# Every eighth gathered row added on VectorE instead of TensorE, with the residual rows kept in SBUF

## What is computed

```python
def block(xb):                      # 128 tokens; 8 heads, 16 experts per head
    ...                             # product keys: scores s1, s2, two rounds of top-16
    g = jax.nn.softmax(sc, axis=-1)
    u = jnp.take(u_tab, eidx, axis=0)
    act = jax.nn.gelu(jnp.einsum('thkd,td->thk', u, xb), approximate=False)
    coef = (g * act.astype(jnp.float32)).astype(xb.dtype)
    return jnp.einsum('thk,thkd->td', coef, jnp.take(v_tab, eidx, axis=0))
...
x = x + _peer(_rmsnorm(x, norm_ffn), w_q, keys1, keys2, u_tab, v_tab)
y = _rmsnorm(x, norm_final)
```

## Time and profile before

| | us |
|---|---|
| Median of 3 runs | 3596.52 (3595.49 to 3606.69) |
| The profiled execution | 3593.31 |
| Its span in the trace | 3591.5 |

### The profile page before, as it was taken

The page is one execution under the profiler, slowest core; times in us unless marked ns, Lnnn a source line. Parts: engine busy times, 40 slices in busy tenths (PEclk is TensorE's granted clock), DMA queues, the critical chain, the costliest instruction groups (busy, mean ns, idle before and its releaser), DMA issues.

```text
span 3591.5 us, 33867 instructions
## 1 busy us (share of the span) xinstructions
PE 3193.5 (89%) x10052; PEld 1819.9 (51%) x10052; DVE 2417.2 (67%) x5507; ACT 1431.2 (40%) x4220; POOL 1381.5 (38%) x1231
## 2 busy tenths in 40 slices
PE   7889998999999998999999998989999877777776
PEld 6676555555555555555655555555555322222232
DVE  6633579767656678867656588867656666666664
ACT  4312444554334345554334345553333333333332
POOL 2101345333333445434333345434343444444443
PEclk9899999999999999999999999999999999999999
DMA  4256999999999999999999998999999999999998
GB/s 135 71 170 230 382 418 343 381 415 369 418 411 408 399 411 345 392 392 392 419 405 398 401 407 336 401 386 400 418 411 400 416 419 420 396 420 401 419 381 347
DMA packets 232072, 1336.42 MB, mean 372 GB/s; under 512 B 27664, under 2 KB 49296, under 8 KB 92624
## 3 DMA queue, kind: packets, MB, share of 16 engines
q0 software_dynamic: 156672, 1140.92, 78.1%
q1 hardware_dynamic: 62992, 179.96, 13.5%
q10 hardware_dynamic: 12224, 13.38, 1.0%
HBM read 1310.93 MB, written 23.23 MB: 371 GB/s over the span
## 4 chain that ended last, share of the span: by engine, by line
PE 58%; DMA 21%; DVE 8%; ACT 8%; issue 4%; POOL 1%; POOLq 0%; SPq 0%; ACTq 0%; DVEq 0%
PE ps_acc L765 32%; DMA rows<-in_experts,idx 20%; PE ps_a L593 14%; PE ps_v L593 4%; PE ps_a L668 3%; DVE rows L1383 3%; ACT uy L824 2%; POOL rows L1510 1%; DVE va L1228 1%; ACT coef L918 1%; ACT diag L922 1%; PE ps_a L695 1%; PE ps_y L635 1%; ACT L915 1%; PE ps_a L672 1%
## 5 line engine op out<-in xcount | busy, mean ns | idle before, releaser
L765 PE MATMUL ps_acc<-rows,diag 128*128 128x512 f32 x4352 | 2030.9, 614 | 292.0 <-ACT diag L922 289.3
L1510 POOL DMA_INDIRECT rows<-in_experts,idx x1088 | 1257.3, 1156 | 1894.5 <-PE ps_acc L765 1529.2
L1383 DVE CUSTOM_DVE_ANT_0 rows<-rows,xn 128x1024 f32<-128x1024 f32 x1088 | 1330.1, 1232 | 827.4 <-DMA rows<-in_experts,idx 812.7
L765 PEld LDWEIGHTS ps_acc<-rows,diag 128*128 128x128 f32 x4352 | 831.2, 196 | 1335.8 <-issue 848.0
L915 ACT ACTIVATE act_v<-dots 128x2 f32<-128x2 f32 x544 | 109.6, 201 | 1161.2 <-DVE dots L1383 1150.0
L922 ACT ACTIVATE diag<-pk,coef 128x128 f32<-128x128 f32 x1088 | 377.2, 394 | 17.7
L593 PE MATMUL ps_a<-xnT,ring 128*128 128x272 f32 x1536 | 375.8, 400 | 0.9 <-ACT xnT L812 0.7
L593 PEld LDWEIGHTS ps_a<-xnT,ring 128*128 128x128 f32 x1536 | 297.4, 194 | 93.3 <-issue 34.4
L918 ACT ACTIVATE coef<-act_v,soft 128x1 f32<-128x1 f32 x1088 | 261.4, 287 | 17.8
L593 PE MATMUL ps_a<-gates,ring 128*128 128x272 f32 x1024 | 247.7, 395 | 4.4 <-issue 3.5
L1228 DVE SCALAR_TENSOR_TENSOR va<-va,pk 128x302 f32<-128x302 f32 x480 | 240.2, 564 | 1.9
(11 more groups left out here) (227 smaller groups left out, 2258.9 us busy)
## 6 DMA issues: line engine op xcount, KB each, us to landing
ring<-in_slabs SPq DMA_DIRECT2D x256, 512.0 KB
rows<-in_experts,idx POOLq DMA_INDIRECT x1088
ring<-made_slabs SPq DMA_DIRECT2D x24, 512.0 KB
sc<-score_rows SPq DMA_DIRECT2D x68, 128.0 KB
score_rows<-gp ACTq DMA_DIRECT2D x32, 256.0 KB
xt<-in_x_prompt SPq DMA_DIRECT2D x4, 1024.0 KB, 14.4
x_rows<-xt ACTq DMA_DIRECT2D x4, 1024.0 KB, 10.8
x2t<-x_rows SPq DMA_DIRECT2D x8, 512.0 KB
```

What stands on the lines that cost most here:

```text
L765: ins = pe.matmul(ps_acc[:, h, :], diag[:, slot, :], rows[:, slot, D + h * 512:D + (h + 1) * 512], start=False, stop=False, skip_group_che ...
L1383: ins = dve.tensor_tensor_reduce(rows[:, slot, 0:D], rows[:, slot, 0:D], xn[:, :], 1.0, 0.0, ALU.mult, ALU.add, dots[:, s:s + 1])
L1510: pool.indirect_dma_start(out=rows[:, slot, :], out_offset=None, in_=experts, in_offset=bass.IndirectOffsetOnAxis(ap=idx[:, a, k:k + 1], a ...
```

## The change

The residual rows get two buffers by tile parity (`x2t[:, t % 2, :]`), and stay out of PE: `start` of PE is gone, and PE's first slot of a tile starts the accumulation (`start=first`). In the prompt tiles the slots with s % 8 == 7 (`added`) have no `diag` and no PE product. DVE adds them to `x2t` with one `scalar_tensor_tensor` (`v` half times coefficient plus `x2t`), after the first two dot products of the following turn (after all four in a tile's first turn). This buffer of the ring has a semaphore of its own, `last_free`. At a tile's end DVE adds `ps_acc` and `x2t` into `yt` once both have all slots (`y_sum`), and PE waits for that before its next tile. The squares are then taken from `yt` (ACT, at the end of the tile's first turn), mean and scaling by DVE at the end of turns 1 and 2, and the inverse root is a power on POOL instead of ACT's root and DVE's reciprocal. SP loads rows at turn 3 instead of 1, with another condition, and stores at turn 3 instead of 0.

```diff
+ADDED = RING - 1
-        x2t = sb("x2t", [P, D])
+        x2t = sb("x2t", [P, 2, D])
...
+        def added(n, s):
+            return n < TILES * TPAIRS and s % RING == ADDED
...
             def rows_free(t):
-                sp.wait_ge(acc_begun, t + 1)
-                pass_wait()
-                sp.wait_ge(xn_ready, t + 1)
-                pass_wait()
+                if t >= 2:
+                    sp.wait_ge(y_sq, t - 1)
+                    pass_wait()
...
-                if ended_at(turn) is not None:
-                    store(ended_at(turn))
+                if turn > 32 and turn % 32 == 3:
+                    store(turn // 32 - 1)
...
-            def start(t):
-
-                w = DEC if t == TILES else P
-                pe.wait_ge(x2_in, loads_of(t))
-                pe.wait_ge(y_ready, t + 1)
-                for h in range(2):
-                    last = pe.matmul(ps_acc[:, h, :], eye[0:w, :], x2t[0:w, h * 512:(h + 1) * 512],
-                                     start=True, stop=False, skip_group_check=True)
-                last.then_inc(acc_begun, 1)
...
             def slots(n, s0, s1):
                 for s in range(s0, s1):
-                    slot = s % RING
-                    pe.wait_ge(diag_done, PAIR * n + s + 1)
+                    if added(n, s):
+                        continue
+                    slot, first = s % RING, s == 0 and n % TPAIRS == 0
+                    if first and n:
+                        pe.wait_ge(y_sum, n // TPAIRS)
+                    pe.wait_ge(diag_done, summed(n, s) + 1)
...
-                    ins.then_inc(slot_free, 1)
+                    ins.then_inc(last_free if slot == ADDED else slot_free, 1)
...
             def end_squares(t):
-
-                steps = PAIR * (TILES * TPAIRS + SPAIRS) if t == TILES else PAIR * TPAIRS * (t + 1)
-                act.wait_ge(y_out, 16 * t + 16)
-                act.wait_ge(slot_free, RING + steps)
-                act.activation(yt[:, :], flat(ps_acc[:, :, :]), ACT.Square, accum_out=fin[:, 0:1]).then_inc(y_sq, 1)
+                act.wait_ge(y_sum, t + 1)
+                act.activation(x2t[:, t % 2, :], yt[:, :], ACT.Square, accum_out=fin[:, 0:1]).then_inc(y_sq, 1)
...
+            def add_slot(n, s):
+
+                dve.wait_ge(coef_done, PAIR * n + s + 1)
+                x2 = x2t[:, n // TPAIRS % 2, :]
+                mark(dve.scalar_tensor_tensor(x2, rows[:, ADDED, D:2 * D], coef[:, s:s + 1], x2, ALU.mult, ALU.add))
+                after(count[0])
+                dve.sem_inc(last_free, 1)
...
             def end(t):
...
+                dve.wait_ge(y_out, 16 * t + 16)
...
+                dve.tensor_tensor(yt[:, :], flat(ps_acc[:, :, :]), x2t[:, t % 2, :], ALU.add).then_inc(y_sum, 1)
...
+            def end_scale(t):
+
+                dve.wait_ge(y_std, t + 1)
+                dve.scalar_tensor_tensor(yt[:, :], yt[:, :], fin[:, 2:3], gl[:, :], ALU.mult, ALU.mult).then_inc(y_ready, 1)
...
                     dot(n, STEPS * r, STEPS * r + BATCH)
+                    if added(*earlier):
+                        add_slot(*earlier)
...
+            def end_root(t):
+
+                pool.wait_ge(y_ms, t + 1)
+                pool.tensor_tensor(fin[:, 2:3], fin[:, 1:2], half[:, 0:1], ALU.pow).then_inc(y_std, 1)
...
-                    pool.wait_ge(slot_free, PAIR * n + s + 1)
+                    if slot == ADDED:
+                        pool.wait_ge(last_free, rounds(n, s) + 1)
+                    else:
+                        pool.wait_ge(slot_free, (RING - 1) * rounds(n, s) + slot + 1)
```

More of the change, by code:

```diff
@@ L375, in loads_of, with summed, rounds @@
             return 16 * (TILES + 2) if t == TILES else 16 * t + 16
+        def added(n, s):
+            return n < TILES * TPAIRS and s % RING == ADDED
+        def summed(n, s):
+            whole, part = min(n, TILES * TPAIRS), n - min(n, TILES * TPAIRS)
+            return whole * (PAIR - PAIR // RING) + part * PAIR + (s - s // RING if n < TILES * TPAIRS else s)
+        def rounds(n, s):
+            return PAIR // RING * n + s // RING
         def by_step(ap):
@@ L510, in _ @@
                 beside(2 * turn)
+                if k == 3 and g < GROUPS:
+                    load_rows(2 * g + 1)
                 if k == 1 and g < GROUPS:
-                    load_rows(2 * g + 1)
                     sp.wait_ge(score_out[1], 128 * g + 64)
@@ L774, in _ @@
             pe.wait_ge(kept_in, 16)
-            pe.sem_inc(slot_free, RING)
-            pe.sem_inc(acc_begun, 1)
+            pe.sem_inc(slot_free, RING - 1)
+            pe.sem_inc(last_free, 1)
             pe.sem_inc(y_done, 2)
@@ L788, in _ @@
                     beside(2 * turn + 1)
-                    start(turn // 32)
                     slots(n, s, s + STEPS)
@@ L978, in _ @@
                 if turn % 32 == 0:
-                    if t is not None:
-                        end_squares(t)
                     beside(2 * turn)
-                    if t is not None:
-                        end_root(t)
                     pair_start(n, r)
@@ L990, in _ @@
                 batch(n, TB * r + 1)
+                if t is not None:
+                    end_squares(t)
                 beside(2 * turn + 1)
             end_squares(TILES)
-            end_root(TILES)
         @block.vector
@@ L1401, in end, with end_mean @@
             def end(t):
-                dve.wait_ge(y_sq, 1 * t + 1)
+                last = (LAST_PAIR, PAIR - 1) if t == TILES else (TPAIRS * (t + 1) - 1, PAIR - 2)
+                dve.wait_ge(y_out, 16 * t + 16)
+                dve.wait_ge(slot_free, RING - 1 + summed(*last) + 1 - (rounds(last[0] - TILES * TPAIRS, last[1]) + 1 if t == TILES else 0))
+                dve.wait_ge(last_free, 1 + rounds(*last) + 1)
+                dve.tensor_tensor(yt[:, :], flat(ps_acc[:, :, :]), x2t[:, t % 2, :], ALU.add).then_inc(y_sum, 1)
+            def end_mean(t):
+                dve.wait_ge(y_sq, t + 1)
                 dve.tensor_scalar(fin[:, 1:2], fin[:, 0:1], 1.0 / D, EPS, ALU.mult, ALU.add).then_inc(y_ms, 1)
-                dve.wait_ge(y_std, 1 * t + 1)
-                step(dve.reciprocal(fin[:, 3:4], fin[:, 2:3]))
-                dve.scalar_tensor_tensor(yt[:, :], flat(ps_acc[:, :, :]), fin[:, 3:4],
-                                         gl[:, :], ALU.mult, ALU.mult).then_inc(y_ready, 1)
+            def end_scale(t):
+                dve.wait_ge(y_std, t + 1)
+                dve.scalar_tensor_tensor(yt[:, :], yt[:, :], fin[:, 2:3], gl[:, :], ALU.mult, ALU.mult).then_inc(y_ready, 1)
             setup_constants()
@@ L1432, in _ @@
                     weights(n)
+                earlier = (n, STEPS * r - 1) if r else (n - 1, PAIR - 1)
                 if turn % 32 == 0:
                     dot(n, STEPS * r, STEPS * (r + 1))
+                    if n and added(*earlier):
+                        add_slot(*earlier)
                     if ended_at(turn) is not None:
@@ L1445, in _ @@
                         choose(n + 1, r)
+                if turn > 32 and turn % 32 == 1:
+                    end_mean(turn // 32 - 1)
+                if turn > 32 and turn % 32 == 2:
+                    end_scale(turn // 32 - 1)
             end(TILES)
+            end_mean(TILES)
+            end_scale(TILES)
         @block.gpsimd
@@ L1537, in _ @@
                         ahead(n, r, b)
+                if turn > 32 and turn % 32 == 1:
+                    end_root(turn // 32 - 1)
+            end_root(TILES)
 def _lay_out(inputs):
```

15 lines of the change are left out of this document (7 added, 8 removed).

## The result

| | before | after |
|---|---|---|
| median of 5 runs each | 3596.52 us (3591.29 to 3606.69) | 3612.71 us (3609.31 to 3622.93) |
| ratio after / before | | 1.0048, 95% interval 1.0027 to 1.0068 |
| profiled execution: time, span | 3593.31, 3591.5 us | 3619.37, 3617.4 us |

The change costs 17 us (0.0048 x 3596), where 33 us of gain were forecast. The time is 7 us above the range that was given. In the next fences the columns are those of the same views of before.

The account below looks back on a forecast made before the run. The prediction took PE to bound some windows and transfers, at about 420 GB/s, the rest. Its terms, 28 + 15 + 4 - 13 - 0.9 = 33 us gained, gave 3560.3 us (3563.5 on the median's scale), range 3540 to 3585; whole range 3500 to 3606.

Parts of the forecast that it names:

- (1): PE loses 128 slots, 239 us of its work; 28 us gained in windows with PE full and rate under 410 GB/s.
- (4): Serial stretch from 1380 to 1440 us, PE's small products alternating with ACT's copies: 4 us gained.
- (3): DVE's added slots cost time only where DVE is the bound, in three groups: 13 us lost.
- (2): Tile ends: PE starts its next slot sooner, 2.8 us at five ends, 0.5 at three: 15 us gained.
- the very end: At the kernel's end the sum and POOL's power stay on the path, the table load goes: 0.9 us lost.
- A: Rival: relief spreads through a fuller ring of gathers, giving half the cap, 87 us: 3510 us; chance 0.18.
- D: Rival: PE's gaps grow and its clock falls, eating into (1); no size, counted inside B.
- (5): New waits, DVE for ACT's coefficient and slot 7's later release by DVE, cause no stall: cost 0.
- Rival C: DVE becomes the bound of the first stretch; 48 adds at 1.5 us cost 72 us: 3622 us; chance 0.17.
- B: Rival: no difference, as mixing work sets the stretches below 420 GB/s; 4 us gained, 3592.5 us; chance 0.21.
- B's second mechanism: Added DVE operations delay POOL's gather issues by 0.9 us each, 115 us in all, a twelfth of it counting: 8 us.
- 420 GB/s cap: Transfer ceiling, largest 20 us window 422; all that can be won is 173 us, down to 3066 us.

Follow-up runs that it names:

- e1: The change with all 128 added slots given back to PE, new tile end kept; 3575.9 us, 0.9948 of before.
- e5: The change with the 128 slots added by nobody; PE skips them and releases their buffer; 3585.8 us, 0.9966 of before.
- e13: The change with only the last added slot of each tile (8 of 128) back on PE, sum still late; 3594.8 us, 0.9994 of before.
- e9: As e5, but PE does a product of zeros in each left-out slot's place, restoring its load; 3570.9 us, 0.9945 of before.
- e14: As e5, but with a finished tile's sum behind two dot products instead of four; 3575.0 us, 0.9949 of before.
- e8: As e1, but with a finished tile's sum behind two dot products instead of four; 3573.6 us, 0.9939 of before.
- e10: As e5, but gathering only half the bytes of the left-out slots, 67 MB fewer; 3464.1 us, 0.9636 of before.
- e11: As e9, but gathering only half the bytes of the same slots, 67 MB fewer; 3505.2 us, 0.9757 of before.
- e4: The change with 36 of 128 added slots, those in pairs 1 to 3 of three groups, back on PE; 3592.6 us, 0.9992 of before.
- e12: e4 and e7 together: 92 adds, added slot and sum behind two dots at a tile's start; 3578.7 us, 0.9958 of before.
- e7: The change with added slot and sum behind two dots instead of four in a tile's first turn; 3591.2 us, 0.9988 of before.
- e2: The change with each add cut from 1024 to 8 columns, all waits and releases kept; 3584.2 us, 0.9965 of before.
- e6: As e1, but slot 7's gather also waits for DVE's release after an idle 8-column operation; 3584.3 us, 0.9966 of before.

## Why the prediction was wrong

The ratios add up along one path of runs, by construction:

| part | forecast, us | measured, us |
|---|---|---|
| new tile end, no adds (before to e1) | 15 + 5 x 1.29 = 21 gain | 18.7 ± 7.5 gain |
| (1), (4) relief of PE (e1 to e5) | 28 + 4 = 32 gain | 6.5 ± 9 loss |
| (3) 120 adds elsewhere (e5 to e13) | 13 loss | 10 ± 8 loss |
| 8 adds before a sum (e13 to after) | 5 x 1.29 = 6 loss, inside (2) | 19.4 ± 9.5 loss |
| the very end | 0.9 loss | not resolved |
| sum | 33 gain | 17.3 ± 7.4 loss |

(1) is the step that failed, and with it the sign. Its first half held: windows at 418 to 420 GB/s kept their rate with a freer PE. Its second half took a window of 20 us with PE busy for over 18.6 us and a rate under 410 as one in which PE is the limit and will give back an eighth of its slot work. The runs show that it isn't: where 32 us of gain were forecast, the relief gave losses of 7.5 ± 9 and 3.6 ± 11 us, with either order of the sum (e5 against e9, e14 against e8), and a gain of 44 ± 10 us only when transfers were cut (e10 against e11). Being full of work and being what the rest waits for are two things. The lower bound of (1), 0, was the value to take. (4) was part of the same reasoning and falls with it. Rivals A and D: A (relief spreads) is excluded by e5, and the first stretch moves 391 GB/s, where A wanted over 407. D was right that PE's freed time shrinks with the clock, and gave no size: it is 100 of 239 us.

(2) had the right mechanism, and its gain is real (e1). Its pace was about right: PE's first slot comes 2.5 us sooner at a tile start on the mean, where the forecast has 2.8 at five and 0.5 at three. (By its own rows, 3091.33 - 3088.4, the 2.8 is 2.9.) The missed part is that this was counted as time, while POOL's next gathers are held by slot 7 until the add is done; two turns on, all but 0.5 us of it is gone. The adds in front of the sums were priced at 1.29 us each, in the five tile ends that counted, and all eight cost 2.4 ± 1.2.

(3) was not far off. The 120 other adds cost 10 us, 13 forecast. The crowded turn whose timeline is shown above takes 15.2 us in before, from its first dot at 1348.72 to the next turn's at 1363.90, and 20.4 in after (1361.73 to 1382.16), so 5 us in one turn where 3 to 5 had been expected of the whole stretch. But e1 takes 17.4 us for the same turn (1348.48 to 1365.83), so 2 of the 5 are there without any add. Which of them cost is less sure: by e4 the 36 in crowded pairs cost 20 ± 9, by e12 11 ± 7.

(5) was right on the coefficient (5.2 us of wait in all) and wrong on slot 7. "This matters only if it comes after the release of the next slot" was the right test, answered from the order of the code rather than from a row: in after POOL waits for it 79 times, 200 us. Most of that wait is not time lost: e7 keeps 189 us of it and is 21.6 us faster, e2 keeps 138 us at the ratio of e5, and e6 with 80 us of it is 6.5 ± 9 us over e1.

Rival C, slower through DVE, had the sign right and the place partly: time is lost on DVE's path, part of it in crowded pairs as C said (e4, e12), but by e13 19 ± 9.5 us of it at eight tile starts that C did not look at. In the traces the three tiles with crowded parts (first, third, fifth) take 33 us longer in after than in before, and the other three of that stretch 4 us less; e1 without adds has 21 more and 19 less. So against e1 the adds cost about as much in the crowded three (12 us) as in the other three (15 us), each read from one trace. C's 48 adds at 1.5 us, 72 us, are far too many. B's mechanism, stretches bound by mixing work, fits the relief's zero, but no run tests it, and the 44 us of e10 against e11 speak against it as the whole story. In B's second mechanism "the twelfth" of 128 is a fourteenth (9 of 128); its 8 us are right. That second mechanism, the Trainium skill's rule (GPSIMD Engine Reference, Specifications) on shared SBUF interfaces, agrees with after in its direction: a gather's issue takes 1194 ns on the mean (L1546), against 1171 in e5, which has no adds, and 1156 in before; runs without adds spread from 1164 (e1) to 1178 (e9). 23 ns x 1088 is 25 us of POOL's time, a fifth of the 115 us that the prediction worked with, and none of it was shown to be on the path. The 420 GB/s cap stood within 1%: the highest 20 us windows are 422 in after, 423 in e10 and 424 in e1 and e5, which is over the 422 that was named as its limit, but not by an amount that changes the sum. e10's 119 us for 67 MB is three quarters of what the cap would give.

## What to carry to other kernels

Taking work off an engine that is busy 89% of the time was worth nothing here while a second limit stood as near; before costing such a relief, find the limit by cutting the other resource (here the bytes), not by how full the engine looks in a window. When work moves to another engine, look first at the few places where that engine stands in front of a hand-over: here 8 of 128 adds cost 19 ± 9.5 us and the other 120 cost 10 ± 8. Before a longer operation is blamed on the work added beside it, look for it in a run without that work; the slow taps are in e1 too. And a change with several parts should be taken apart: its better half alone, the new tile end with all slots on PE and an early sum, runs 0.6% faster than before.

## What was not expected of the hardware

Less work on PE lowered the clock granted to it, from 0.970 to 0.943 over the span, and from 0.98 to 0.91 in the window of 2820 to 3078 us, and each matmul record took 639 ns in place of 614; of the 239 us that 128 slots kept PE busy only 139 came off the group (2030.9 to 1892.0 us). e9, whose filler product gives PE the load back, returns to 0.968 and 620 ns. And a tap of the convolution (128 x 302) took 0.47, 0.91 or 0.97 us (four in 1.86 in before, 3.63 in after and 3.86 in e1), without any change to the tap and, in e1, without any change to its place in DVE's order.
